# Prompt attention of a hybrid decoder step: the probabilities are turned by a product with a diagonal matrix instead of a transpose

## What is computed

```
s_s = einsum('bqgrd,bqgkcd->bqgrkc', q, kb) * scale
p_s = masked_softmax(s_s, m_s)
o_s = einsum('bqgrkc,bqgkcd->bqgrd', p_s, vb)
s_w = einsum('bqgrd,bkgd->bqgrk', q, kw) * scale
p_w = masked_softmax(s_w, m_w)
o_w = einsum('bqgrk,bkgd->bqgrd', p_w, vw)
return gate[..., 0:1] * o_c + gate[..., 1:2] * o_s + gate[..., 2:3] * o_w
```

## Time and profile before

| | |
|---|---|
| median of 3 runs | 1466.07 us (1464.58 to 1468.4) |
| profiled execution | 1465.81 us, its span 1464.1 us |
| PE busy | 1430.9 us (98%) |
| DVE busy | 847.9 us (58%) |
| ACT busy | 413.0 us (28%) |
| POOL busy | 211.9 us (14%) |
| mean granted clock of TensorE | 0.996 |

### The profile page before, as it was taken

The page is one execution under the profiler, slowest core; times in us unless marked ns, Lnnn a source line. Parts: engine busy times, 40 slices in busy tenths (PEclk is TensorE's granted clock), DMA queues, the critical chain, the costliest instruction groups (busy, mean ns, idle before and its releaser), DMA issues.

```text
span 1464.1 us, 30419 instructions
## 1 busy us (share of the span) xinstructions
PE 1430.9 (98%) x12340; PEld 1130.4 (77%) x12340; DVE 847.9 (58%) x1649; ACT 413.0 (28%) x890; POOL 211.9 (14%) x276
## 2 busy tenths in 40 slices
PE   9999999999999999999999889999999999999997
PEld 8887578878888866775667668888888888888886
DVE  7665058633433447526774537677666766666664
ACT  3112372123333316227775631102311011101001
POOL 1000324532222224434001210000000000000000
PEclk9999999999999999999999999999999999999999
DMA  6222543211111238457003963432222222222221
GB/s 264 87 87 72 182 166 111 96 61 44 50 46 36 101 118 254 156 165 250 1 2 91 334 260 137 141 98 83 75 84 86 76 83 87 87 74 97 90 87 61
DMA packets 57399, 163.94 MB, mean 112 GB/s; under 512 B 7312, under 2 KB 19696, under 8 KB 55952
## 3 DMA queue, kind: packets, MB, share of 16 engines
q1 hardware_dynamic: 48608, 121.46, 24.9%
q0 software_dynamic: 7936, 39.40, 7.8%
q10 hardware_dynamic: 720, 1.16, 0.2%
HBM read 144.01 MB, written 22.15 MB: 113 GB/s over the span
## 4 chain that ended last, share of the span: by engine, by line
PE 91%; DVE 4%; ACT 2%; issue 1%; SPq 1%; DMA 1%; DVEq 0%; ACTq 0%
PE acc L1059 26%; PE acc L1210 17%; PE acc L1978 5%; PE acc L2006 5%; PE acc L1987 5%; PE acc L2031 4%; PE acc L1152 2%; PE acc L1332 2%; PE acc L1167 2%; PE acc L1733 2%; PE acc L1745 2%; PE acc L1756 1%; PE acc L1349 1%; PE acc L1094 1%; PE acc L1071 1%
## 5 line engine op out<-in xcount | busy, mean ns | idle before, releaser
L1059 PE MATMUL acc<-sb_work,sb_ring 128*128 128x272 f32 x602 | 150.9, 392 | 0.0
L2524 ACT ACTIVATE sb_omemT<-acc 128x272 f32<-128x272 f32 x74 | 29.3, 396 | 386.0 <-PE acc L1978 234.2
L1210 PE MATMUL acc<-sb_work,sb_ring 128*128 128x272 f32 x504 | 129.2, 398 | 4.4 <-DVE sb_work L2733 2.9
L1059 PE MATMUL acc<-sb_work 128*128 128x272 f32 x530 | 133.0, 393 | 0.0
L1059 PEld LDWEIGHTS acc<-sb_work,sb_ring 128*128 128x128 f32 x602 | 114.4, 190 | 23.6
L1059 PEld LDWEIGHTS acc<-sb_work 128*128 128x128 f32 x530 | 100.5, 190 | 21.4 <-issue 0.8
L1210 PEld LDWEIGHTS acc<-sb_work,sb_ring 128*128 128x128 f32 x504 | 93.1, 190 | 25.7 <-issue 7.1
L1978 PE MATMUL acc<-sb_work,sb_ring 128*128 128x272 f32 x308 | 77.2, 393 | 1.0 <-issue 1.0
L1987 PE MATMUL acc<-sb_work,sb_ring 128*128 128x272 f32 x308 | 77.1, 392 | 0.0
L1210 PE MATMUL acc<-sb_onsaT,sb_omemT 128*128 128x272 f32 x272 | 69.5, 399 | 0.0
L1978 PEld LDWEIGHTS acc<-sb_work,sb_ring 128*128 128x128 f32 x308 | 58.4, 190 | 13.4 <-issue 1.4
(11 more groups left out here) (495 smaller groups left out, 2787.4 us busy)
## 6 DMA issues: line engine op xcount, KB each, us to landing
sb_ring<-w_stream SPq DMA_DIRECT2D x144, 512.0 KB, 3.5
sb_work<-pages SPq DMA_DIRECT2D x56, 192.0 KB, 4.2
branch_gates<-sb_work SPq DMA_DIRECT2D x24, 272.0 KB, 2.8
sb_work<-branch_gates POOLq DMA_DIRECT2D x8, 816.0 KB, 14.7
sb_ring<-w_stream SPq DMA_DIRECT2D x16, 384.0 KB, 3.3
sb_work<-mem_kT SPq DMA_DIRECT2D x8, 512.0 KB, 7.5
sb_work<-mem_v SPq DMA_DIRECT2D x8, 512.0 KB, 9.9
query_features<-sb_work SPq DMA_DIRECT2D x10, 272.0 KB, 3.5
```

The costliest lines, as they stand in the source:

```text
L1059: mm = pe.matmul(out, w[:, q, :], x[q], start=q == 0, stop=q == n - 1)
L1210: mm = pe.matmul(acc[3][:, (7 * u + ph) % 2, 0:HALF_T], w, x, start=q == 0 and ph in (0, 1, 5), stop=q == 3, skip_group_check=True)
L2524: act.activation(keeps(u)[:, s], bank(u, (0, 3)[s]), ACT.Copy).then_inc(unit_kept, 1)
```

## The change

The probabilities stay as the exponential left them. Instead DVE writes, for each group and branch of the unit, a matrix of 128 x 128 with the factors of gate over sum on its diagonal: the identity, broadcast over the matrices, times the factors, broadcast over the columns, in one operation into `scale_diag[:, u % 3]`. PE takes each block of probabilities as the weights of an ordinary f32 product with the matrix of its group and branch, which gives the transposed and scaled block in one step. The three buffers of `scale_diag` lie at `late_at`, under `m_probT`, whose own addresses stay. Since that place holds rows on their way to memory, DVE now waits for both `spilled` semaphores behind its first maximum.

```diff
--- before.py
+++ after.py
@@ -329,7 +329,8 @@
         bf_causal = region(None, P // 2).bitcast(BF16)
         bf_cmp = region(None, QT * NC_P // 2).bitcast(BF16)
         late_at = at[0]
-        m_probT = [region(None, MEM_H * 2, P) for _ in range(2)]
+        scale_diag = region(late_at, 3, 2 * NG, P)
+        m_probT = [region(late_at + n * MEM_H * 2 * P, MEM_H * 2, P) for n in range(2)]
         assert at[0] <= 16800
         smp1 = 16800
         w1_two = region(smp1 + 7168, 2, CMP // 2, P)
@@ -1742,7 +1743,8 @@
                     pe.wait_ge(at_copied, u)
                 for g in range(NG):
                     for k in range(len(bs) * (t + 1)):
-                        mm = pe.transpose(acc[2][:, g, k * P:(k + 1) * P], probs[u % 3][:, g, k * P:(k + 1) * P], ident)
+                        mm = pe.matmul(acc[2][:, g, k * P:(k + 1) * P], probs[u % 3][:, g, k * P:(k + 1) * P],
+                                       scale_diag[:, u % 3, g * len(bs) + k // (t + 1), :], start=True, stop=True)
                 mm.then_inc(at_turn, 1)
 
             def att_values(u):
@@ -3027,14 +3029,8 @@
                 own(dve.reciprocal(rows(8), rows(4)))
                 own(dve.tensor_tensor(rows(12).rearrange("p (g b) -> p g b", g=NG),
                                       rows(8).rearrange("p (g b) -> p g b", g=NG), gates, ALU.mult))
-                if nb == 2:
-                    shown = probs[u % 3][:, :, 0:nb * w].rearrange("p g (b k) -> p g b k", b=nb)
-                    ins = dve.tensor_tensor(shown, shown, bc(rows(12).rearrange("p (g b) -> p g b", g=NG), 3, w), ALU.mult)
-                else:
-                    for g in range(NG):
-                        ins = dve.tensor_scalar(probs[u % 3][:, g, 0:w], probs[u % 3][:, g, 0:w],
-                                                small[:, c + 12 + g:c + 13 + g], None, ALU.mult)
-                ins.then_inc(at_scaled, 1)
+                dve.tensor_tensor(scale_diag[:, u % 3, 0:NG * nb, :], bc(ident, 1, NG * nb), bc(rows(12), 2, P), ALU.mult)\
+                   .then_inc(at_scaled, 1)
 
             def att_out(r):
                 dve.wait_ge(at_pv, HEAD_UNITS * (r + 1))
@@ -3042,6 +3038,8 @@
 
             page_copy(0)
             att_max(0)
+            for n in range(2):
+                dve.wait_ge(spilled[n], 16 * N_FILL // 2)
             for u in range(1, N_ATT + 1):
                 if u < N_ATT:
                     att_max(u)
```

## The result

The changed kernel takes 1492.37 us (median of 4 runs, 1489.09 to 1494.07) against 1465.32 us (4 runs) for the kernel before: a ratio of 1.0181, 95% interval 1.0152 to 1.021. Run again in five rounds beside the kernel before it was 1491.26 us at a ratio of 1.0172, interval 1.0159 to 1.0185, which is +25 us. The forecast was 1490.

What follows compares the result with a forecast made beforehand. The prediction took TensorE's own work to bound the prompt attention: +27.0 us for products less 3.0 given back by VectorE makes +24.0 on 1465.81 us, so 1490 us, range 1486 to 1496.

Steps and rivals of the forecast that it cites:

- TensorE sets the pace of this stretch: Prompt attention, first scores to last products: TensorE busy 108.06 of 110.90 us, VectorE close behind, ScalarE with room.
- The product has two records, and the second costs 0.1125 us: Transposes of 240 probability blocks become f32 products, 480 records for 240: +27.0 us, bounds 25.9 and 29.4.
- The pair that it was read from: Memory attention in the earlier trace: eight transposes in 0.88 us beside eight f32 products in 1.78 us.
- the holes: TensorE's waits for VectorE's scaling before two transpose groups of each steady head: 0.46 us a head, 2.3 in five.
- VectorE's relief gives back 3.0 us: Attention: diagonals replace scaling in place, so TensorE waits less; 2.3 us steady plus 0.7 first head, bounds 1.5 and 3.5.
- TensorE's later arrival: Attention: each product takes longer before the next scores, so VectorE also gets more time; no size of its own.
- The new wait costs nothing: VectorE's wait for spilled rows behind its first maximum: stores landed near 656.8 us, ten us of cover, no cost.
- No new wait on ScalarE: ScalarE's copies and exponentials in the attention: no wait grows, since its work fits into some 135 us.
- a product costs no more than a turn: Rival, attention blocks: product as cheap as the transpose, about 2 us added, 3.0 given back, 1465 us; chance 0.04.
- Four turns for a product: Rival, attention blocks: four passes where the transpose makes one, 79.2 us less 3.0, 1542 us; chance 0.02.
- A new wait on a copy or an exponential: Rival, ScalarE in the attention: falls behind by one 1.025 us copy a head, 6.2 us more, 1496 us; chance 0.08.

Runs made afterwards that it cites:

- double_turn: The kernel before with every transpose of a probability block issued twice and no product; ratio 1.0145 to the kernel before.
- double_diag: The changed kernel with every diagonal matrix written twice by VectorE; ratio 1.0194 to the kernel before.
- diag_turned: The changed kernel with plain transposes for the products, diagonals still written, scaling left out of the output; 1463.79 us, ratio 0.9979 to the kernel before.
- ident_product: The kernel before with each transpose made an ordinary f32 product with the identity, VectorE scaling in place; 1491.18 us, ratio 1.0170.
- half_product: The changed kernel with products for the first group's blocks only, the second group's plainly transposed and unscaled; ratio 1.0092 to the kernel before.
- group_signal: The kernel before without diagonals, VectorE scaling and counting group by group, TensorE waiting for each group's count; 1463.92 us, ratio 0.9972.
- bf16_product: The changed kernel with probabilities and diagonal matrices in bf16; 1454.06 us, ratio 0.9907 to the kernel before.

## Why the prediction was right, point by point

*TensorE sets the pace of this stretch.* Shown: double_turn adds nothing but TensorE records and costs 23.0 us in the attention, double_diag adds 18.5 us of VectorE's work and leaves the steady head at 21.48 us.

*The product has two records, and the second costs 0.1125 us.* The count of 480 was right. The price is 0.119 us in place, which makes 6 x 4.75 = 28.5 us instead of 27.0, within the bounds of 25.9 and 29.4; the whole stretch has 139.20 - 111.13 = 28.1 between the changed kernel and diag_turned. The pair that it was read from the earlier trace rows gave the right rule and a size some 5% too small. For this and the holes below, the head came out at 21.48 us where 21.3 was said.

*VectorE's relief gives back 3.0 us.* Measured without the product, in diag_turned: 3.3 us in all, within the bounds of 1.5 and 3.5. It is 0.56 a head instead of 0.46, 2.8 in five heads, because the prediction counted the holes alone and not that the turns behind them get shorter too; some 0.5 are left for the first head, where 0.7 was estimated. Both terms were a little too small, by 1.1 us in 27.0 and by 0.3 in 3.0, and as they have opposite signs 0.8 remains: +24.8 in the attention, where the sum had +24.0. That the errors partly cancel is luck, but each term was within its own bounds. The prediction named both VectorE's relief and TensorE's later arrival as what closes the holes; diag_turned and ident_product show that either is enough.

*The new wait costs nothing.* Right within 0.1 us, once, and diag_turned, which has it as well, is faster than before.

*No new wait on ScalarE.* Right: its copies wait longer for TensorE than before, not the other way.

*The rivals.* That a product costs no more than a turn is ruled out for f32 (0.119 us more); a bf16 product costs less than an f32 turn, but no run has a bf16 turn beside it. Four turns for a product is ruled out by the same number. A new wait on a copy or an exponential is ruled out by the chain and by TensorE's waits for copies, 0.2 us before and after.

The Trainium skill's rule (Perfetto Trace Analysis, section Transposes: use a transpose where one is meant, not a standard matmul) holds in f32 by these numbers. Eight bf16 products in 0.55 us against eight f32 turns in 0.97 don't test it, since the format differs as well.

What stays open is what makes up the last tenth of the product's price, whether half_product's medians are above the line for the clock alone, and how often the clock falls in the first head; single traces can't tell.

## What to carry to other kernels

Before moving work from one engine to another, see which of the two has the idle time: here 13 us less of VectorE's work (71.88 for 85.04) were worth 3.3 us, and the product that replaced them cost 28.1 on an engine that was idle for 2.84 of 110.90 us. A product that stands in for a transpose should be priced by its records: here an f32 product has two of them where the transpose has one, and a bf16 one has a single short one. The same idea loses 25 us in f32 and gains 14 with bf16 probabilities, of which an unknown part would come from bf16 transposes as well. The small holes in front of the busy engine could be closed here by a finer count (one for each group, group_signal) instead of less work.

## What the runs showed of the hardware

The granted clock of TensorE fell to the 1.2 GHz level in the first head in three of the ten traces: from 672.0 to 675.4 us in half_product, from 674.1 to 677.5 in double_diag and from 674.9 to 678.2 in bf16_product (means of 0.86 and 0.72 over 672 to 676 and 676 to 680 us). Each time TensorE had waited right before or in that window. But the other traces have idle time much alike and stay at 1.00: in the kernel before TensorE was busy for 2.40 of 4.00 us from 668 to 672, in half_product for 2.60. So what tells the one execution from the other isn't shown. By the sums above the fall costs 1.4 to 1.5 us (half_product, double_diag) out of at most 1.7. An added wait ahead of such a place may therefore cost more than its own length, in some executions only; that a wait brings the fall about is not shown.
